# A fifth place for the query weight slices of a hybrid decoder step, and ScalarE's query copies put ahead of the splits

## The reference

```python
x = x + jnp.concatenate([ya, yb], axis=-1) @ w_o          # pooling heads and attention heads
x = x + peer(rms_norm(x, norm2_g), w_pq, sub_keys, expert_u, expert_v)

def peer(h, w_pq, sub_keys, expert_u, expert_v):
    q = (hf @ w_pq).reshape(N, PEER_HEADS, 2, PEER_HALF)   # 8 heads x 2 halves x 128
    s = jnp.einsum('nhcd,hckd->nhck', q, sub_keys)
    sv, si = lax.top_k(s, PEER_TOPK)
    ...                                                     # top 16 of the pairs, softmax g
    a = gelu(x_t . expert_u[eidx]);  out = (g * a) @ expert_v[eidx]
```

## Time and profile before

| | |
|---|---|
| median of 3 runs | 981.31 us (981.14 to 981.70) |
| the profiled execution, its own time | 981.55 us |
| its span in the trace | 980.1 us |
| outside the span | 1.45 us |
| TensorE busy | 958.2 us, 98% |
| VectorE, ScalarE, GpSimd busy | 777.5, 558.6, 438.6 us |
| TensorE's granted clock | 1.00 of full speed in every slice |

### The profile page before, as it was taken

The page is one execution under the profiler, slowest core; times in us unless marked ns, Lnnn a source line. Parts: engine busy times, 40 slices in busy tenths (PEclk is TensorE's granted clock), DMA queues, the critical chain, the costliest instruction groups (busy, mean ns, idle before and its releaser), DMA issues.

```text
span 980.1 us, 19215 instructions
## 1 busy us (share of the span) xinstructions
PE 958.2 (98%) x6440; PEld 835.3 (85%) x6440; DVE 777.5 (79%) x1805; ACT 558.6 (57%) x1092; POOL 438.6 (45%) x328
## 2 busy tenths in 40 slices
PE   5999999999999999999999999999999999999998
PEld 2347879899999999999999998888888888888887
DVE  2569987269999948999999976777888878788873
ACT  2023354454445559999999975654555555555552
POOL 4643465145788776776777770011212211131200
PEclk9999999999999999999999999999999999999999
DMA  9635748668855554444445456797888888888872
GB/s 330 149 109 160 238 139 308 209 226 316 280 176 175 180 185 150 152 161 160 150 155 165 151 173 217 257 337 283 300 300 305 299 279 296 303 304 303 291 263 94
DMA packets 75424, 221.24 MB, mean 226 GB/s; under 512 B 11301, under 2 KB 23725, under 8 KB 74964
## 3 DMA queue, kind: packets, MB, share of 16 engines
q1 hardware_dynamic: 60812, 179.12, 53.7%
q0 software_dynamic: 12800, 40.36, 13.3%
q10 hardware_dynamic: 1744, 0.92, 0.4%
HBM read 217.41 MB, written 3.14 MB: 225 GB/s over the span
## 4 chain that ended last, share of the span: by engine, by line
PE 86%; DVE 4%; DMA 4%; ACTq 2%; ACT 2%; issue 2%; SPq 0%; DVEq 0%
PE psum L1123 33%; PE psum L1059 22%; PE psum L1060 12%; PE psum L1071 3%; PE psum L1055 3%; PE psum L603 3%; PE psum L872 2%; ACTq L402 1%; PE psum L873 1%; DMA w_raw<-expert_v 1%; DMA rows_in<-expert_u,eidx 1%; PE psum L581 1%; DMA w_raw<-expert_ut 1%; DVE work L1825 1%; PE psum L887 1%
## 5 line engine op out<-in xcount | busy, mean ns | idle before, releaser
L1630 POOL TENSOR_TENSOR w_lo<-w_raw,w_hi 128x1024 fp32r<-128x1024 f32 x116 | 279.1, 2410 | 124.1 <-ACT w_hi L1170 123.9
L1059 PE MATMUL psum<-h_split,w_hi 128*128 128x256 f32 x1792 | 327.0, 284 | 1.3 <-issue 1.3
L1060 PE MATMUL psum<-h_split,w_lo 128*128 128x256 f32 x1024 | 289.4, 283 | 0.0
L1059 PEld LDWEIGHTS psum<-h_split,w_hi 128*128 128x128 f32 x1792 | 279.2, 192 | 2.6 <-issue 1.4
L1170 ACT ACTIVATE w_hi<-w_raw 128x1024 fp32r<-128x1024 f32 x214 | 224.9, 1051 | 39.4 <-DMA w_raw<-expert_ut 27.6
L1060 PEld LDWEIGHTS psum<-h_split,w_lo 128*128 128x128 f32 x1024 | 196.1, 191 | 0.0
L2145 DVE TENSOR_TENSOR w_lo<-w_raw,w_hi 128x1024 fp32r<-128x1024 f32 x98 | 120.5, 1229 | 54.7 <-ACT w_hi L1170 54.4
L1123 PE MATMUL psum<-w_hi,ag_hi 128*128 128x512 f32 x512 | 158.2, 390 | 0.4 <-DVE ag_lo L2152 0.4
L1123 PE MATMUL psum<-w_hi,ag_lo 128*128 128x512 f32 x512 | 158.0, 389 | 0.0
L1170 ACT ACTIVATE ag_hi<-store 128x256 fp32r<-128x256 f32 x128 | 53.2, 417 | 152.5 <-PE psum L1123 152.4
L1123 PEld LDWEIGHTS psum<-w_hi,ag_hi 128*128 128x128 f32 x512 | 95.8, 188 | 20.6 <-ACT w_hi L1170 0.8
(11 more groups left out here) (347 smaller groups left out, 1485.0 us busy)
## 6 DMA issues: line engine op xcount, KB each, us to landing
w_raw<-expert_ut SPq DMA_DIRECT2D x128, 512.0 KB
w_raw<-expert_v SPq DMA_DIRECT2D x86, 512.0 KB
raw_more<-expert_v SPq DMA_DIRECT2D x42, 512.0 KB, 4.8
w_slice<-w_pq_cols SPq DMA_DIRECT2D x32, 512.0 KB, 5.3
w_most<-w_in_blocks SPq DMA_DIRECT2D x8, 699.0 KB, 11.3
w_slice<-w_o_half SPq DMA_DIRECT2D x8, 512.0 KB, 4.7
v_cache<-cache_v POOLq DMA_DIRECT2D x64, 64.0 KB, 3.7
w_o_sb<-w_o_half SPq DMA_DIRECT2D x8, 512.0 KB, 6.1
```

Of the source, the lines that this page charges most:

```text
L1059: pe.matmul(out, w_hi[:, s, c, :], h_split[:, c, a], start=(c == 0 and a == 0), stop=False)
L1060: mm = pe.matmul(out, w_lo[:, s, c, :], h_split[:, c, 0], start=False, stop=(c == KC - 1), skip_group_check=wide)
L1630: pool.tensor_tensor(w_lo[:, s], w_raw[:, s], w_hi[:, s].bitcast(F32), ALU.subtract).then_inc(S["w_lo_ready"], 1)
```

## The change

A fifth place for slices, `w_slice_x`, is laid over `probT`, whose first use (the prompt's transposed probabilities) is over when `prompt_values(1)` is done (`yb_psum` 2), and whose second use comes after slice 9 (`copy_sT(1)`). The table `R_SLOT` gives the place of each slice: 0 to 4 in turn for the first ten, 0 to 3 for the next four, then 0 and 1. So slices 5 to 9 are loaded one product earlier relative to their use than before, as are 10 to 13; slice 4 is loaded right behind slice 0, ahead of 1, 2 and 3. SP's order changes with it: each part of `w_o_sb` now follows slice 7 + i, and not 6 + i, and the first four sample slices wait for the last product in their place (`rq(14)`, `rq(15)`, `rq(12)`, `rq(13)`, in this order; before `rq(12)` to `rq(15)`).

In ScalarE's program `copy_q(r - 3)` now stands ahead of `high_q(r)`, for r = 3 to 7, and the later copies stand likewise. `high_q(11)` moves ahead of the second `rs_copy`. Nothing that is computed changes.

```diff
--- before.py
+++ after.py
@@ -202,6 +202,8 @@
     sr_s = at("sr_s", cur[0], [P, 4, NK])
     h_rows = at("h_rows", cur[0], [NS, D])
     probT = take("probT", [P, NPG, P])
+    w_slice_x = at("w_slice_x", cur[0] - NPG * P, [P, KC, P])
+    q_lo_x = at("q_lo_x", cur[0] - NPG * P, [P, KC, P], F32R)
     ys_rows = take("ys_rows", [P, 2, HD])
     wo_rows = take("wo_rows", [P, 2, P])
     assert cur[0] <= Z0
@@ -331,7 +333,7 @@
     h_save = nc.dram_tensor("h_save", [NS, D], F32, kind="Internal").ap()
 
     S = Named(nc, ctx)
-    w_slice_in = [ctx.enter_context(nc.semaphore(f"w_slice_in{i}")) for i in range(SLICES)]
+    w_slice_in = [ctx.enter_context(nc.semaphore(f"w_slice_in{i}")) for i in range(SLICES + 1)]
     row_in = [ctx.enter_context(nc.semaphore(f"row_in{i}")) for i in range(2)]
     v_more_in = [ctx.enter_context(nc.semaphore(f"v_more_in{i}")) for i in range(2)]
     w_in_ring = [ctx.enter_context(nc.semaphore(f"w_in_ring{i}")) for i in range(RING)]
@@ -345,9 +347,28 @@
         i = r % 3 if r < 9 else (r - 9) % 2
         return q_hi_x[:] if i == 2 else q_hi_ab[:, i]
 
+    R_SLOT = (0, 1, 2, 3, 4, 0, 1, 2, 3, 4, 0, 1, 2, 3, 0, 1)
+    assert len(R_SLOT) == RSLOTS and KC == 2 * SLICES
+
+    def r_turn(r):
+
+        return (2 if R_SLOT[r] < SLICES else 0) + R_SLOT[:r + 1].count(R_SLOT[r])
+
+    def s_turn(i, j):
+
+        return 2 + R_SLOT.count(j) + i + 1
+
+    def before(r):
+
+        return max([x for x in range(r) if R_SLOT[x] == R_SLOT[r]], default=-1)
+
+    def q_raw(r):
+
+        return w_slice[:, R_SLOT[r]] if R_SLOT[r] < SLICES else w_slice_x[:]
+
     def q_low(r):
 
-        return q_lo[:, (KC + r) % SLICES]
+        return q_lo[:, R_SLOT[r]] if R_SLOT[r] < SLICES else q_lo_x[:]
 
     def bc(ap, axis, n):
         a = ap.unsqueeze(axis)
@@ -459,21 +480,30 @@
 
             sp.dma_start(pool_sample[0, :, 0:NST - DS, :], state_pool[0, :, DS:NST, :]).then_inc(S["out_done"], 16)
 
-            Q_PQ, Q_SAMPLE = KC, KC + RSLOTS
-
             def load_slice(q):
 
-                old = q - SLICES
-                if old >= Q_SAMPLE:
-                    sp.wait_ge(S["rq_s_psum"], (old - Q_SAMPLE) // 4 + 1)
-                elif old >= Q_PQ:
-                    sp.wait_ge(S["rq_psum"], old - Q_PQ + 1)
-                elif old >= 4:
-                    sp.wait_ge(S["wo_psum"], 2 * (old - 4) + 2)
-                elif old >= 0:
-                    sp.wait_ge(S["wo_half"], old + 1)
-                src = w_o_half[q] if q < Q_PQ else w_pq_cols[(q - Q_PQ) % RSLOTS]
-                sp.dma_start(w_slice[:, q % SLICES], src).then_inc(w_slice_in[q % SLICES], 16)
+                if q >= SLICES:
+                    sp.wait_ge(S["wo_half"], q - SLICES + 1)
+                sp.dma_start(w_slice[:, q % SLICES], w_o_half[q]).then_inc(w_slice_in[q % SLICES], 16)
+
+            def load_q(r):
+
+                if r < SLICES:
+                    sp.wait_ge(S["wo_psum"], 2 * r + 2)
+                elif before(r) < 0:
+                    sp.wait_ge(S["yb_psum"], 2)
+                else:
+                    sp.wait_ge(S["rq_psum"], before(r) + 1)
+                sp.dma_start(q_raw(r), w_pq_cols[r]).then_inc(w_slice_in[R_SLOT[r]], 16)
+
+            def load_sample(i):
+
+                for j in range(SLICES):
+                    if i:
+                        sp.wait_ge(S["rq_s_psum"], i)
+                    else:
+                        sp.wait_ge(S["rq_psum"], max(r for r in range(RSLOTS) if R_SLOT[r] == j) + 1)
+                    sp.dma_start(w_slice[:, j], w_pq_cols[SLICES * i + j]).then_inc(w_slice_in[j], 16)
 
             def k_loads(first, n):
                 page_loads(sp, first, cache_kt, kT[:].rearrange("p b k -> p (b k)"), PAGE, S["k_in"], n)
@@ -491,8 +521,10 @@
             for q in range(EARLY, 4):
                 load_slice(q)
             k_loads(32, K_SP - 32)
-            for q in range(4, 12):
+            for q in range(4, KC):
                 load_slice(q)
+            for r in (0, 4, 1, 2, 3):
+                load_q(r)
             sp.wait_ge(S["zp_copied"], 8)
             sp.wait_ge(S["rope_done"], 3)
             sp.wait_ge(S["idx_rope_done"], 3)
@@ -505,14 +537,14 @@
             for b in range(DB):
                 sp.dma_start(pool_sample[0, b, NST - DS:NST, :], z[b * DS:(b + 1) * DS, 2, 0:PW]
                              ).then_inc(S["rows_out"], 16)
-            for q in range(12, 14):
-                load_slice(q)
+            for r in (5, 6):
+                load_q(r)
             sp.wait_ge(S["log_g_done"], 2)
             for i in range(8):
-                load_slice(14 + i)
+                load_q(7 + i)
                 sp.dma_start(w_o_sb[:, i].rearrange("p a k j -> p (a k) j"), w_o_half[i]).then_inc(S["w_o_in"], 16)
-            for q in range(22, Q_SAMPLE):
-                load_slice(q)
+            for r in range(15, RSLOTS):
+                load_q(r)
 
             def load_u(row, slot):
                 sp.dma_start(w_raw[:, slot], expert_ut[bass.ds(row, 1)].rearrange("a p c j -> p (a c) j")
@@ -531,15 +563,12 @@
             sp.wait_ge(S["wo_s_psum"], 1)
             for s in range(RING):
                 load_u(s, s)
-            for q in range(Q_SAMPLE, Q_SAMPLE + SLICES):
-                load_slice(q)
+            load_sample(0)
             for n in range(FRONT):
                 sp.wait_ge(S["prod_done"], n + 1)
                 load_u(n + RING, n % RING)
                 if n % 4 == 1 and n < 12:
-                    q = Q_SAMPLE + SLICES * (n // 4 + 1)
-                    for i in range(SLICES):
-                        load_slice(q + i)
+                    load_sample(n // 4 + 1)
                 if n == 8:
                     sp.wait_ge(S["rows_copied"], 2)
                     sp.dma_start(h_save, h_rows[:]).then_inc(S["h_saved"], 16)
@@ -998,7 +1027,7 @@
                 if i == 0:
                     pe.wait_ge(S["h2_s_ready"], 1)
                 for j in range(4):
-                    slice_in(KC + RSLOTS + 4 * i + j)
+                    pe.wait_ge(w_slice_in[j], 16 * s_turn(i, j))
                 if i:
                     pe.wait_ge(S["rq_s_copied"], i)
                 for k in range(KC):
@@ -1290,10 +1319,10 @@
 
             def high_q(r):
 
-                act.wait_ge(w_slice_in[(KC + r) % SLICES], 16 * ((KC + r) // SLICES + 1))
+                act.wait_ge(w_slice_in[R_SLOT[r]], 16 * r_turn(r))
                 if 3 <= r < 13:
                     act.wait_ge(S["rq_psum"], r - 1 if r >= 11 else r - 2)
-                copy(q_high(r), w_slice[:, (KC + r) % SLICES]).then_inc(S["q_hi_ready"], 1)
+                copy(q_high(r), q_raw(r)).then_inc(S["q_hi_ready"], 1)
 
             for i, c in enumerate(CHUNKS):
                 act.wait_ge(S["x1_prompt"], i + 1)
@@ -1344,24 +1373,22 @@
             high_q(2)
             copy_log(0)
             copy_log(1)
-            for r in range(3, 7):
+            for r in range(3, 8):
+                copy_q(r - 3)
                 high_q(r)
-                copy_q(r - 3)
-            high_q(7)
-            copy_q(4)
             act.wait_ge(S["rows_out"], 16 * (9 + 1 + DB))
             rs_copy(act, copy, 0)
+            copy_q(5)
             high_q(8)
-            copy_q(5)
             sample_exp(0)
+            copy_q(6)
             high_q(9)
-            copy_q(6)
+            copy_q(7)
             high_q(10)
-            copy_q(7)
             sample_exp(1)
             copy_q(8)
+            high_q(11)
             rs_copy(act, copy, 1)
-            high_q(11)
             copy_q(9)
             copy_sT(0)
             copy_sT(1)
@@ -1602,7 +1629,7 @@
             def low_q(r):
 
                 pool.wait_ge(S["q_hi_ready"], r + 1)
-                pool.tensor_tensor(q_low(r), w_slice[:, (KC + r) % SLICES], q_high(r).bitcast(F32), ALU.subtract
+                pool.tensor_tensor(q_low(r), q_raw(r), q_high(r).bitcast(F32), ALU.subtract
                                    ).then_inc(S["q_lo_pool"], 1)
 
             def join_sq(i):
@@ -1915,7 +1942,7 @@
             def low_q(r):
 
                 dve.wait_ge(S["q_hi_ready"], r + 1)
-                dve.tensor_tensor(q_low(r), w_slice[:, (KC + r) % SLICES], q_high(r).bitcast(F32), ALU.subtract
+                dve.tensor_tensor(q_low(r), q_raw(r), q_high(r).bitcast(F32), ALU.subtract
                                   ).then_inc(S["q_lo_dve"], 1)
 
             tally(0)
```

## The result

The changed kernel takes 984.06 us (median of 20 runs, 981.88 to 988.9), the kernel before 981.07 (20 runs, 979.04 to 983.36): 1.0034 times as long, interval 1.0025 to 1.0044, or 3.0 us more. The forecast was 981.3 with a range to 982.4, and 5% for slower by over 0.2%. The profiled execution took 983.63 us, its span is 982.1.

A forecast was written before the change was run, and what follows sets the result against it. TensorE, busy 98% of the span, was taken as the bound. Gains of 0.84 and 1.57 less a new wait of 2.36 left 0.05 us, so 981.31 became 981.26, say 981.3, range 980.3 to 982.4.

The forecast's parts named there:

- Part 1: Query stage, copies first and slices earlier: 0.84 us at rs(2) and 1.57 at rs(7), 2.41 gained by rq(9).
- The bound by VectorE: At rq(3): it waits for VectorE's low_q(3), ending at 151.68, so rq(3) stays at 151.78.
- the first place: TensorE's gap of 0.75 us at rs(0): closes, but gains 0; upper bound about 0.36 if VectorE were free earlier.
- Part 2: high_q(11) ahead of the second rs_copy: new TensorE wait in front of rs(8), taking 2.36 of the 2.41 us.
- the cancellation: Gain of 2.41 us against the wait of 2.36 at rs(8), 0.05 left: 980.8 to 981.8, chance 75%.
- Behind that point TensorE meets the schedule of before: After rs(8): products releasing high_q(12) and everything later keep their times; no further wait worth closing in the query stage.
- Part 3: Transfers reordered: cost 0; late sample slices could hold rq_s(0) at 215.96 by up to 1.4 us, that rival 13%.

The follow-up runs named there:

- e10: Changed kernel with second rs_copy again ahead of high_q(11), first four sample slices reordered, VectorE's low_q(3) and low_q(4) ahead of sample selection parts: 979.89 us, ratio 0.9992.
- e1: Changed kernel with the second rs_copy put back ahead of high_q(11): 979.40 us, ratio 0.9989 to the kernel before.
- e1b: Changed kernel with the second rs_copy put back ahead of high_q(11), run a second time unchanged: 979.79 us, ratio 0.9986.
- e4: Kernel before, four places, with only ScalarE's copies put ahead of the splits; second rs_copy stays ahead of high_q(11): 979.64 us, ratio 0.9999.
- e5: Five places and their loads, with ScalarE's order as in the kernel before: 980.15 us, ratio 1.0000.
- e6: Changed kernel with second rs_copy again ahead of high_q(11) and the first four sample slices requested in order of freed places: 979.81 us, ratio 0.9991.
- a1: Changed kernel run again unchanged for a second trace: 982.33 us, one time.
- e3: Kernel before with one edit, high_q(11) ahead of the second rs_copy: 984.29 us, ratio 1.0039.
- e2: Changed kernel with 18 idle matmuls on TensorE between rq(9) and rs(8): 982.84 us, ratio 1.0018.
- e12: Kernel before with 5 and 2 idle matmuls in the two TensorE gaps ahead of the second norm: 980.89 us, ratio 0.9988.
- e8: Changed kernel with one sr copy ahead of high_q(11) and one behind: 982.29 us, ratio 1.0008.
- b2: Kernel before run again unchanged, for a third trace of it: 981.25 us, one time.
- e2b: Changed kernel with 9 idle matmuls on TensorE between rq(9) and rs(8): 982.42 us, ratio 1.0007.

## Why the prediction was wrong

**Part 1, mechanism right, size off.** No `rs` waits for `q_ring`; `rq(9)` starts at 172.86. That is 0.37 behind the forecast 172.49, and the first query product already starts 0.34 later; counted from there the gain is 2.38 in these two traces, against 2.41 forecast. The bound by VectorE held: `low_q(3)` starts at 150.82 and takes 1.22, and `rq(3)` starts 0.10 behind its end, at 152.14, so the first place gained nothing. What makes VectorE late is there again, 2.62 us for the first 128x256 instruction and 0.47 for the next, and e10 moved it away from GpSimd's subtraction and got 0.48; the rule of the Trainium skill cited in the forecast (SBUF — State Buffer, Who interferes with whom) agrees with that once more. The 2.41, though, was read from the one trace of four with the most waiting (2.8 us; the others 1.1, 1.0 and 1.9). The closed stage takes 66.5, that of before 67.9 in the mean of four (67.2 to 68.9), so this term is 1.4 (0.7 to 2.4) by the traces. By the times it may be less: the six sets of runs that close the gaps and have no new wait (e1, e1b, e4, e5, e6, e10) are 0 to 1.4 us faster than before, 0.7 in the mean. The same trace gave both the gap and the base, but the base was then moved to a median in which the gap is smaller.

**Part 2, the wait right, within 0.1.** A gap of 2.1 to 2.4 behind `sr` was forecast; it is 2.27 in after, a1 and e3. It comes from the durations of three instructions of ScalarE and not from a transfer, and so repeats while part 1's gaps don't. Counted from the first product, `rs(8)` is 0.05 later in after than in before, where 0.05 earlier was forecast. That it came so near in these two traces is luck: the cancellation paired a cost that is always paid with a gain at its highest.

**"Behind that point TensorE meets the schedule of before" is the step that failed.** `rs(8)` is 0.39 later than before (178.20 against 177.81), but the last `rs` is 1.9 later in the same two traces (stage starts 0.34 apart, stages 70.4 and 68.9), and the 1.5 between is the clock at 0.50. No rival had the clock. I priced a gap at its own length, when the earlier trace rows with gaps of 1.30 at full clock was no bound for one of 2.27.

**Part 3 right.** `rq_s(0)` starts at 217.99 without a wait, and e6 with earlier slices is not faster.

**The sum again.** +2.3 (wait) + 1.6 (clock, 2.8 - 1.2 of all the runs) - 1.4 (gaps) = 2.5, against 3.0 measured (2.5 to 4.3); with 0.7 for the gaps it would be 3.2. The wait and the clock are shown by e1, e3 and e2; the size of the gaps' part in the medians stays open between about 0 and 1.4. The chances were off by the missing rival and not by noise: 5% for slower stood against a cost of 2.36 that was certain and a gain that was not.

## What to carry to other kernels

A new wait of over 2 us in a TensorE that is otherwise busy can cost more than its length (here five gaps of six were followed by half clock): look at the granted clock of the next 5 us, and give a clock fall a rival of its own. When an edit trades one wait for another, ask of each what sets its length; one set by instructions repeats, one set by a transfer needs several traces before it is booked as gain. A copy whose result the next product needs doesn't go behind an instruction that waits for the product before.

## What was not expected of the hardware

- A gap of 2.27 us lowered the clock in two traces (after, a1) and not in a third (e3); a gap of 1.79 did in e12, one of 1.78 in e8 did not. So in these traces the length alone does not decide. Falls go with length all the same: 5 of the 6 gaps of 2.0 us and more, 1 of 6 between 1.5 and 1.8, 2 of 30 below. The runs say the same, 20 of 20 at 0.998 or less in after and 9 of 12 in e3 against 57 of 116 in before. Why after's gap is followed by a fall more often than e3's of the same length is not shown.
- The fall came late, with TensorE busy again. An estimate from the stretches puts it 1.4 us behind the end of the gap in after, 1.3 in a1, 1.2 in e10, 0.9 in e5, 0.7 in b2 and 0.1 in e12. It lasted 3.4 us in seven traces and 6.8 in e12. In after the halved clock cost 1.5 us: single products took 0.41 us instead of 0.28, and pairs 0.63 instead of 0.40.
- Nine idle matmuls in the gap kept the clock in e2b's trace and took the mean shortfall from 2.8 to 0.7 us. Work that nobody reads can pay, if it is shorter than the wait; the 18 of e2 were not, and gave back part of it.
